# Thirty-nine column orders in the feed-forward products of a hybrid transformer layer

## What is computed

```python
h = rms_norm(x, norm_ffn_g[l])
x = x + jnp.square(jax.nn.relu(h @ w_ff1[l])) @ w_ff2[l]     # w_ff1 2048 x 8192, w_ff2 8192 x 2048
return rms_norm(x, norm_final_g)
```

## Time and profile before

| what | value |
|---|---|
| median of 3 runs | 2856.42 us (2855.27 to 2858.01) |
| the profiled execution | 2856.4 us |
| its span, first to last instruction | 2854.6 us |
| TensorE matmul busy | 2829.1 us, 99% of the span |
| TensorE weight load busy | 2443.2 us, 86% |
| VectorE, ScalarE busy | 1930.7 us (68%), 1355.4 us (47%) |
| DMA engines | about half busy, 177 GB/s |
| granted TensorE clock | 0.998 of full speed |

### The profile page before, as it was taken

The page is one execution under the profiler, slowest core; times in us unless marked ns, Lnnn a source line. Parts: engine busy times, 40 slices in busy tenths (PEclk is TensorE's granted clock), DMA queues, the critical chain, the costliest instruction groups (busy, mean ns, idle before and its releaser), DMA issues.

```text
span 2854.6 us, 38752 instructions
## 1 busy us (share of the span) xinstructions
PE 2829.1 (99%) x15872; PEld 2443.2 (86%) x15872; DVE 1930.7 (68%) x2513; ACT 1355.4 (47%) x1729; POOL 54.3 (2%) x102
## 2 busy tenths in 40 slices
PE   9999999999999999999999999999999999999998
PEld 8899888888888888888888888888888888888887
DVE  7645557678766658888988875456666555656556
ACT  5433654357444446555555544444345434444434
POOL 0000210000000000000000000000000000000000
PEclk9999999999999999999999999999999999999999
DMA  7444344564555544443443355544354555554443
GB/s 279 183 187 163 136 175 178 200 236 167 196 186 187 204 159 160 148 142 140 147 148 133 134 180 201 190 187 157 135 205 179 191 190 193 192 205 179 190 192 148
DMA packets 72849, 506.66 MB, mean 177 GB/s; under 512 B 8384, under 2 KB 8512, under 8 KB 12896
## 3 DMA queue, kind: packets, MB, share of 16 engines
q1 hardware_dynamic: 71136, 497.83, 47.2%
q0 software_dynamic: 1104, 5.90, 0.6%
q10 hardware_dynamic: 432, 0.45, 0.0%
HBM read 499.95 MB, written 2.10 MB: 176 GB/s over the span
## 4 chain that ended last, share of the span: by engine, by line
PE 87%; DVE 7%; ACT 3%; issue 2%; DMA 1%; SPq 0%; POOL 0%; DVEq 0%; ACTq 0%
PE double L1358 81%; PE bank L1358 5%; DVE cacc L2060 2%; DVE wlo L2054 1%; ACT whi L1716 1%; DVE cst L2077 1%; PE bank L1361 1%; DVE Tn L2568 0%; DVE cst L2054 0%; DVE cacc L2057 0%; ACT cacc_r L1919 0%; ACT tmp L1917 0%; DMA mblk<-in_memT 0%; DMA vec<-in_vec 0%; DVE t L2054 0%
## 5 line engine op out<-in xcount | busy, mean ns | idle before, releaser
L1358 PE MATMUL double<-AA,whi 128*128 128x512 f32 (+1 forms) x5008 | 1643.5, 380 | 5.9 <-DVE wlo L2054 3.0
L1716 ACT ACTIVATE whi<-raw 128x1024 fp32r<-128x1024 f32 x926 | 925.7, 1049 | 830.4 <-PE double L1358 802.2
L1358 PE MATMUL double<-AA,wlo 128*128 128x256 f32 (+1 forms) x4624 | 1297.2, 281 | 0.0
L2054 DVE TENSOR_TENSOR wlo<-raw,whi 128x1024 fp32r<-128x1024 f32 (+1 forms) x934 | 1101.5, 1214 | 227.0 <-ACT whi L1716 224.9
L1358 PEld LDWEIGHTS double<-AA,whi 128*128 128x128 f32 x5008 | 916.0, 188 | 184.1 <-DVE wlo L2054 4.7
L1358 PEld LDWEIGHTS double<-AA,wlo 128*128 128x128 f32 x4624 | 874.7, 189 | 1.4
L1358 PE MATMUL double<-whi,AA 128*128 128x512 f32 x1536 | 487.7, 393 | 0.5 <-DVE wlo L2054 0.5
L1358 PEld LDWEIGHTS double<-whi,AA 128*128 128x128 f32 x1536 | 288.5, 188 | 60.5 <-DVE wlo L2054 1.3
L1358 PE MATMUL double<-whi,BB 128*128 128x512 f32 x1024 | 316.7, 389 | 0.0
L1358 PE MATMUL double<-wlo,AA 128*128 128x512 f32 x768 | 299.0, 389 | 0.0
L1358 PEld LDWEIGHTS double<-whi,BB 128*128 128x128 f32 x1024 | 192.2, 188 | 40.1
(11 more groups left out here) (335 smaller groups left out, 1719.3 us busy)
## 6 DMA issues: line engine op xcount, KB each, us to landing
raw<-in_wall SPq DMA_DIRECT2D x462, 1024.0 KB, 4.8
raw<-in_wall SPq DMA_DIRECT2D x9, 256.0 KB, 6.4
X<-in_xT SPq DMA_DIRECT2D x1, 2048.0 KB, 11.3
Mm<-in_memT POOLq DMA_DIRECT2D x1, 2048.0 KB, 15.7
tmp<-rqk POOLq DMA_DIRECT2D x16, 128.0 KB, 2.2
mblk<-in_memT SPq DMA_DIRECT2D x8, 256.0 KB, 5.5
dec<-in_dec POOLq DMA_DIRECT2D x1, 1536.0 KB, 8.8
hs<-in_hsT SPq DMA_DIRECT2D x4, 272.0 KB, 5.3
```

Of the source, the lines that this page charges most:

```text
L1358: return q.matmul(out, lhsT, rhs, start=start, stop=stop, skip_group_check=True)
L1716: q.activation(hi_of(j)[:, c], raw[j % RAW][:, c], ACT.Copy).then_inc(S("w_hi"), 1)
L2054: return q.tensor_tensor(out, a, b, o)
```

## The change

`FEATURE_WAYS` gives 14 of the `f1` pairs a way for the long matmuls and one for the short ones. `TOKEN_WAYS` gives 25 of the `f2` pairs a way, and two marks that say whether the reading (`at_in`) and whether the sums (`at_out`) are walked in it. A way is only another access pattern over the same columns:

- `("runs", r)`: the natural order, written as runs of r columns.
- `("leap", s, r)`: runs of r columns; first every s-th run, then the ones behind them, and so on.
- `("turn", r)`: runs of r columns, taken in turns from the first and the second half (in a long `f1` matmul, from the high and the low part).

Where reading and sums are walked alike, each column lands where it did. In six `f2` pairs only one side is walked, and `layout()` then places the 512 weight columns of these pairs in HBM in the order that undoes it. Number and size of matmuls, weight loads, transfers, semaphores and waits stay as they are, and so do all steps of the other engines.

```diff
+FEATURE_WAYS = {
+    (0, 2): (("turn", 128), ("runs", 16)), (0, 3): (("turn", 32), ("runs", 128)),
+    (1, 0): (("turn", 64), ("leap", 4, 16)), (1, 1): (("runs", 128), ("leap", 8, 16)), (1, 2): (("runs", 64), ("leap", 2, 32)), (1, 3): (None, ("leap", 4, 32)),
+    (2, 0): (("turn", 8), ("leap", 2, 64)), (2, 1): (("runs", 16), ("leap", 2, 8)), (2, 2): (("turn", 64), ("leap", 4, 8)), (2, 3): (None, ("leap", 8, 8)),
+    (3, 0): (("turn", 128), ("leap", 2, 16)), (3, 1): (None, ("runs", 32)), (3, 2): (("turn", 16), ("runs", 8)), (3, 3): (None, ("leap", 4, 16)),
+}
+TOKEN_WAYS = {}
+for n, way in enumerate((("runs", 256), ("runs", 16), ("runs", 64), ("leap", 2, 8), ("leap", 4, 8), ("leap", 8, 8), ("leap", 16, 8), ("leap", 8, 16),
+                         ("leap", 16, 16), ("leap", 2, 32), ("leap", 4, 32), ("leap", 8, 32), ("leap", 2, 64), ("leap", 4, 64), ("leap", 2, 128),
+                         ("turn", 64), ("turn", 32), ("turn", 128), ("leap", 2, 4))):
+    TOKEN_WAYS[divmod(n + 1, 4)] = (way, True, True)
+for n, (way, at_in) in enumerate(((("leap", 2, 16), True), (("leap", 2, 16), False), (("leap", 4, 16), True), (("leap", 4, 16), False),
+                                  (("leap", 2, 8), True), (("leap", 2, 8), False))):
+    TOKEN_WAYS[divmod(n + 21, 4)] = (way, at_in, not at_in)
...
+        def walk(way, x):
+            if way is None:
+                return x
+            form, n = way[0], x.shape[1]
+            if form == "leap":
+                return x.rearrange("p (b s r) -> p s b r", s=way[1], r=way[2])
+            if form == "turn":
+                return x.rearrange("p (a b r) -> p b a r", a=2, r=way[1])
+            return x.rearrange("p (b r) -> p b r", r=way[1])
+        def walk2(way, x):
...
+            if way[0] == "turn":
+                return x.rearrange("p a (b r) -> p b a r", r=way[1])
+            if way[0] == "runs":
+                return x.rearrange("p a (b r) -> p a b r", r=way[1])
...
                     elif kind == "N":
-                        o = out[:, m * 512:(m + 1) * 512]
-                        mm_group(o, hh[:, cs], wh[:, i, :], start=first, stop=False)
-                        mm_group(o, hh[:, cs], wl[:, i, :], start=False, stop=False)
-                        ins = mm_group(o, hl[:, cs], wh[:, i, :], start=False, stop=last)
+                        way, at_in, at_out = TOKEN_WAYS.get(pr["idx"] if pr["tag"] == "f2" else None, (None, False, False))
+                        o, h_, l_ = out[:, m * 512:(m + 1) * 512], wh[:, i, :], wl[:, i, :]
+                        if at_in:
+                            h_, l_ = walk(way, h_), walk(way, l_)
+                        if at_out:
+                            o = walk(way, o)
+                        mm_group(o, hh[:, cs], h_, start=first, stop=False)
+                        mm_group(o, hh[:, cs], l_, start=False, stop=False)
+                        ins = mm_group(o, hl[:, cs], h_, start=False, stop=last)
                     else:
...
-                        mm_group(out[0:n, m * 512:m * 512 + 2 * T], wh[:, i, c], both, start=first, stop=False)
-                        ins = mm_group(out[0:n, m * 512:m * 512 + T], wl[:, i, c], hh, start=False, stop=last)
+                        o, s_ = out[0:n, m * 512:m * 512 + 2 * T], out[0:n, m * 512:m * 512 + T]
+                        long, short = FEATURE_WAYS.get(pr["idx"] if pr["tag"] == "f1" else None, (None, None))
+                        mm_group(walk2(long, two(o)) if long else o, wh[:, i, c], walk2(long, both), start=first, stop=False)
+                        ins = mm_group(walk(short, s_), wl[:, i, c], walk(short, hh), start=False, stop=last)
...
+        part = g[src][0][r:r + kt * P, c0:c0 + ncol]
+        way, at_in, at_out = TOKEN_WAYS.get(idx if tag == "f2" else None, (None, False, False))
+        if at_in != at_out:
+            order_ = np.arange(ncol).reshape(-1, way[1], way[2]).transpose(1, 0, 2).reshape(-1)
+            if at_in:
+                order_ = np.argsort(order_)
+            part = part[:, order_]
```

More of the change, by code:

```diff
@@ L1373, in operand @@
             return AA[:, :, o:o + n]
+        def walk(way, x):
[8 more added lines that the diff above has]
+        def walk2(way, x):
+            if way is None:
+                return x
+            if way[0] == "turn":
+                return x.rearrange("p a (b r) -> p b a r", r=way[1])
+            if way[0] == "runs":
+                return x.rearrange("p a (b r) -> p a b r", r=way[1])
+            return x.rearrange("p a (b s r) -> p s a b r", s=way[1], r=way[2]) if way[0] == "out" else x.rearrange("p a (b s r) -> p a s b r", s=way[1], r=way[2])
         def mm(key):
@@ L2937, in layout @@
         r = r0 + k * kt * P
-        wall[n, :, 0:kt * ncol] = g[src][0][r:r + kt * P, c0:c0 + ncol].reshape(kt, P, ncol).transpose(1, 0, 2).reshape(P, kt * ncol)
+        part = g[src][0][r:r + kt * P, c0:c0 + ncol]
[5 more added lines that the diff above has]
+            part = part[:, order_]
+        wall[n, :, 0:kt * ncol] = part.reshape(kt, P, ncol).transpose(1, 0, 2).reshape(P, kt * ncol)
     vec = np.zeros((P, NVEC), np.float32)
```

## The result

| what | before | after |
|---|---|---|
| median | 2857.22 us (4 runs, 2855.27 to 2858.15) | 2866.06 us (4 runs, 2863.10 to 2867.43) |
| profiled execution, span | 2856.4, 2854.6 us | 2866.8, 2865.0 us |

The ratio is 1.003, with a 95% interval of 1.0018 to 1.0043: the change is 0.3% slower, some 9 us. I had forecast no change. That is wrong by little in time, and it is wrong in one step, the price of the walked reading, which I had put at nothing.

The account below looks back on a forecast made before the run. TensorE, busy for 99% of the span, was taken to bound the kernel. Zero for jumps in the readings and zero for jumps in the sums, added to the profiled 2856.4 us, gave 2856.4 us, range 2850 to 2892.

Parts of the forecast that it names:

- What bounds the kernel: Whole kernel: TensorE busy 99% of the span, so each nanosecond in a feed-forward matmul is one of the kernel.
- Counts and side costs: Feed-forward: 1600 matmuls really reordered, 40,912 jumps in readings and as many in sums; issue, transfers and waits add nothing.
- Term 2: Jumps in the sums written to PSUM: zero; bounds 2.6 us less to 17.1 us more, far end 276.5 us.
- Term 1: Jumps in reading the moving columns of feed-forward matmuls: zero; from zero or 2.6 us less to 17.1 us more.
- "same": Whole kernel: a change under about 0.2%, 5.7 us, or 3.6 ns for each of 1600 matmuls, counts as none.
- The bounds from the stages: Stages `gp` and `k` against `f1`: address matters by -1.6 to +1.7 ns a matmul, -2.6 to +2.7 us over 1600.
- Rival 3: Moving reading and stationary loading meet differently: +8 us, 2864.4 us, chance 0.05; or up to 17 us less, chance 0.08.
- Rival 1: Reading or sums lose a column's slot at each run's end: +17.1 us one side, +34.1 both; chance 0.20.
- Rival 2: Scattered sums go at half pace: 2934.9 us if only runs up to 8, 3132.9 if all; chance 0.07.
- The range: Whole kernel: 2850 to 2892 us, up to one slot for a jump on both sides; forecast's own range 2851 to 2862.

Follow-up runs that it names:

- run 3: `f2` groups with stationary operands shifted or with fewer columns, in natural order and under leaps, compared with natural groups; 2869.64 us, executed once.
- run 6: `f1` groups with stationary operands read 8 to 64 columns further on, plus `f2` groups with leaps and shifts, compared with natural groups; 2862.42 us, executed once.
- run 5: The same leaps, reading and sums walked alike, placed behind different neighbouring groups, compared with natural groups; 2863.24 us, executed once.
- run 10: Kernel before, with T products' stationary operands at 192 and 0 bytes, N products walked 4 by 8, first six matmuls of each run 2 by 8; 2859.28 us, 1.0009.
- run 1: Changed kernel with only the sums walked, in all 39 groups, and reading in natural order; 2857.72 us, 1.0003 of the kernel before.
- run 7: Kernel before, with stationary operands of all T products 192 bytes into `whi` and 0 into `wlo`, in place of 0 and 64; 2839.61 us, ratio 0.9941.
- run 4: Survey of leaps in `f2` groups, some in reading or sums alone, runs down to two columns, compared with natural groups; 2940.74 us, executed once.

## Why the prediction was wrong

- **What bounds the kernel: right.** TensorE alone; each nanosecond in a group came through, and no cover was there.
- **Counts and side costs: right.** Issue, transfers, the other weights' order: the one-sided sum pairs (which have all three) and the "runs" token groups cost 0.03 us at most.
- **Term 2, the sums, zero: right**, and now shown, down to runs of two columns.
- **Term 1, the reading, zero: this is the step that failed.** I took it from the delta rule's stepped passes, which read at half the pace, and carried it over to full pace, where no row had more than one jump. At full pace the 14 short-run token groups came to +6.2 us and the feature groups to +2.0 us, 8.3 us or 5.2 ns for each of 1600 reordered matmuls, where "same" allowed 3.6. The pace of jumps that I had matched (1.7 ns) was not the thing that counts. What the runs showed in its place is a cost that belongs to the way, of either sign, and that changes with the address of the stationary operand (runs 3 and 6) and with what ran before (runs 5 and 10).
- **The bounds from the stages** `gp` and `k` were read as -1.6 to +1.7 ns a matmul. They are averages: within `gp`, in the kernel before, a long and a short matmul together take anything from 343 to 357 ns in a fixed turn, by their starts in the trace. And `k` is of form W, three matmuls of 272 columns, which no feed-forward product is, so that it does not compare addresses alone, as I had said. The bounds showed the right mechanism and understated its size: the ways of the change came to between -6.7 and +32 ns in the token groups.
- **Rival 3 was what happened**: I wrote that by 5 ns a matmul to one side it would be +8 us, and gave that 0.05 because I expected the costs to average out. They do so in part (one group gained 0.32 us), but natural order is itself one of the shorter meetings: of the token ways only 4 by 8 was shorter, and most were longer. Nothing in the working could tell which side they would tend to. **Rival 1** would have given (3, 1) with seven jumps 0.14 us and (4, 3) 2.5 us, and gave 0.04 and 0.21. **Rival 2** is refuted, since the sums cost nothing in run 1.
- **The range held by luck.** 2866 us lies in 2850 to 2892, but above 2862 that range was there for rival 1, a slot lost at each jump, which is not what happened.

What stays open: where and by what rule the two readings meet (that their addresses count together is shown, that SBUF is the place is theory A's guess), why 2 by 16 costs some 13 ns with almost any stationary operand, and what the 13.3 ns of natural order are. They are not a floor, since 4 by 8 halves them.

## What to carry to other kernels

Where TensorE is the bound with full-pace float32 products, the order in which the moving columns are read and the addresses of both operands within 256 bytes can matter: from -3% to +16% of a matmul here with runs of 32 bytes and more, and more than double with runs of 8 bytes. The order in PSUM was free. Measure it by stretches of equal matmuls, and after any change ahead of them again, since the same instructions settle into a longer or a shorter rhythm by what ran before. Here 192 bytes of placement and one access pattern took 1.1% off a kernel that was 99% busy.

## What the runs showed of the hardware

- Loading a stationary operand and streaming the moving one are not independent: 64 bytes in the stationary address took a natural 512-column matmul from 226.7 to 233.3 ns (run 3), and 192 bytes in the high and 0 in place of 64 in the low part an `f1` pair of matmuls from 346.7 to 340 ns (run 7).
- The 512-column matmul at full pace took 220 ns in the shortest rhythm seen, 226.7 in natural order, and 451 ns where it read 2 by 2, in runs of 8 bytes (run 4).
- A natural `f2` group stood at 226.7 ns again within its first dozen matmuls in every run. Natural `f1` groups did not always come back: those of block 1 in run 3 stayed at 353.3 ns a pair, in place of 346.7. 4 by 8 has two steady values, 220.0 and 230.6 ns.
- Sums in runs of two columns to stepped PSUM addresses: 226.7 ns, as in one sweep (run 4).
